# Side rows gathered into one run per fast tile, the running sum in two banks by turns, a third copy buffer

## The reference, cut to what matters

```python
def swiglu(h, w_gate, w_up, w_down):
    return (jax.nn.silu(h @ w_gate) * (h @ w_up)) @ w_down

x = x + 0.5 * swiglu(rms_norm(x, ffn1_norm[l]), ffn1_wg[l], ffn1_wu[l], ffn1_wd[l])
```

## Time and profile before

| quantity | value |
|---|---|
| median of three runs | 2538.85 us |
| the profiled execution | 2539.22 us |
| its span | 2537.4 us |
| TensorE busy | 2515.2 us, 99% of the span |
| VectorE busy | 1875.9 us, 74% |
| ScalarE busy | 1162.6 us, 46% |
| mean granted TensorE clock | 0.999 |

### The profile page before, as it was taken

How to read it: one execution, slowest core, us unless ns; L and a number is a source line. 1 busy time by engine, 2 the same in 40 slices (tenths; PEclk the granted TensorE clock), 3 DMA queues, 4 the chain that set the end, 5 groups by cost and what they waited for, 6 DMA issues and landing times.

```text
span 2537.4 us, 35107 instructions
## 1 busy us (share of the span) xinstructions
PE 2515.2 (99%) x13914; PEld 2186.0 (86%) x13914; DVE 1875.9 (74%) x2579; ACT 1162.6 (46%) x1843; POOL 303.0 (12%) x250
## 2 busy tenths in 40 slices
PE   8999999999999999999999999999999999999999
PEld 7899988888999889999888899997888888788887
DVE  8878877777788677887776778877999786642433
ACT  5444445444444444443553444445577535431332
POOL 4000001320000000000023000000286231100001
PEclk9999999999999999999999999999999999999999
DMA  5333333232333333333423233334332333233332
GB/s 155 98 94 99 99 102 92 76 101 79 104 98 107 114 88 94 100 97 112 108 59 100 84 99 100 97 108 130 82 76 72 125 92 110 83 107 100 92 100 83
DMA packets 489961, 248.32 MB, mean 98 GB/s; under 512 B 41921, under 2 KB 486598, under 8 KB 489542
## 3 DMA queue, kind: packets, MB, share of 16 engines
q1 hardware_dynamic: 489346, 245.76, 33.5%
q10 hardware_dynamic: 452, 0.32, 0.1%
HBM read 241.84 MB, written 4.19 MB: 97 GB/s over the span
## 4 chain that ended last, share of the span: by engine, by line
PE 92%; DVE 4%; ACT 2%; DMA 1%; issue 1%; POOL 0%; DVEq 0%; ACTq 0%
PE bank L725 8%; PE bank L727 8%; PE bank L726 8%; PE bank L804 7%; PE bank L806 7%; PE bank L805 7%; PE psS L829 4%; PE psS L830 4%; PE psS L831 4%; PE psT L725 4%; PE psT L727 4%; PE psT L726 4%; PE psT L875 2%; PE psT L877 2%; PE psT L876 2%; PE psS L725 1%
## 5 line engine op out<-in xcount | busy, mean ns | idle before, releaser
L2001 DVE TENSOR_TENSOR wlo<-raw,whi 128x1024 fp32r<-128x1024 f32 (+1 forms) x274 | 362.8, 1326 | 114.7 <-ACT whi L1426 111.5
L725 PE MATMUL bank<-xhi,whi 128*128 128x512 f32 x888 | 349.4, 393 | 1.4 <-issue 1.4
L726 PE MATMUL bank<-xlo,whi 128*128 128x512 f32 x888 | 345.9, 390 | 0.0
L727 PE MATMUL bank<-xhi,wlo 128*128 128x512 f32 x888 | 345.8, 389 | 0.0
L1426 ACT ACTIVATE whi<-raw 128x1024 fp32r<-128x1024 f32 (+1 forms) x271 | 276.8, 1025 | 130.4 <-PE psT L727 92.4
L1458 ACT ACTIVATE whi<-tw 128x1024 fp32r<-128x1024 f32 x128 | 135.8, 1061 | 271.7 <-PE bank L806 158.9
L804 PE MATMUL bank<-xsh,whi 128*128 128x256 f32 x768 | 216.7, 282 | 1.6 <-issue 1.6
L806 PE MATMUL bank<-xsh,wlo 128*128 128x256 f32 x768 | 217.3, 283 | 0.0
L805 PE MATMUL bank<-xsl,whi 128*128 128x256 f32 x768 | 217.2, 283 | 0.0
L829 PE MATMUL psS<-hhi,whi 128*128 128x512 f32 x512 | 202.3, 395 | 0.0
L830 PE MATMUL psS<-hlo,whi 128*128 128x512 f32 x512 | 202.2, 395 | 0.0
(11 more groups left out here) (586 smaller groups left out, 6424.7 us busy)
## 6 DMA issues: line engine op xcount, KB each, us to landing
raw<-in_ffn_wg SPq DMA_DIRECT2D x88, 512.0 KB
raw<-in_ffn_wu SPq DMA_DIRECT2D x88, 512.0 KB
raw<-in_w_mlp SPq DMA_DIRECT2D x64, 512.0 KB
raw<-in_w_in SPq DMA_DIRECT2D x53, 512.0 KB
raw<-in_ffn_wd SPq DMA_DIRECT2D x48, 256.0 KB
raw<-in_ffn_wd SPq DMA_DIRECT2D x32, 384.0 KB
raw<-in_ffn_wd SPq DMA_DIRECT2D x48, 192.0 KB
raw<-in_ffn_wd SPq DMA_DIRECT2D x48, 128.0 KB
```

Of the source, the lines that this page charges most:

```text
L725: pe.matmul(dest, a, rhs_hi(k), start=start and k == 0, stop=False)
L726: pe.matmul(dest, a, rhs_lo(k), start=False, stop=False)
L727: mm = pe.matmul(dest, b_, rhs_hi(k), start=False, stop=stop and k == tiles - 1)
L2001: dve.tensor_tensor(wlo[:, a:a + n], raw[:, a:a + n], whi[:, a:a + n].bitcast(F32), ALU.subtract).then_inc(s_split, 1)
```

## The change

It does four things. The four side halves become two whole units that stand together (`side` in place of `side_half`), between P5 and P6, so TensorE's list becomes P1 to P5, unit 0, unit 1, P6, P7. The growing sum lies in bank 0 in even windows and in bank 2 in odd ones, so P1 waits only for work of the window before last. The copy after P3 gets its own buffer, `part[2]`. On ScalarE the copy after P5 moves ahead of `sums_hi(w+1, 0)` and `whole_hi(w+1, 0)`; on VectorE line 2158 moves ahead of `whole_lo(w, 1)`, and line 2172 ahead of `side_adds(w, 0)` and `whole_lo(w+1, 0)`. `s_used` counts as follows: P4 one, unit 0 one, P6 two.

```diff
@@ -166,7 +166,7 @@
         cwl = sb("cwl", 2 * S, F32R)
         dwh = sb("dwh", S, F32R)
         dwl = sb("dwl", S, F32R)
-        part = [sb(f"part{i}", QT) for i in range(2)]
+        part = [sb(f"part{i}", QT) for i in range(3)]
         assert at[0] <= nc.sbuf_usable_end, (at[0], nc.sbuf_usable_end)
         top = at[0]
 
@@ -812,11 +812,8 @@
                 def summed(j):
                     return lambda k: (xsh[:, (4 * k + j) * QT:(4 * k + j + 1) * QT], xsl[:, (4 * k + j) * QT:(4 * k + j + 1) * QT])
 
-                def side_half(w, i, half):
-                    unit = SIDES[w][i]
-                    cut = (len(unit) + 1) // 2
-                    for j in (range(cut, len(unit)) if half else range(cut)):
-                        grp, m, k = unit[j]
+                def side(w, i):
+                    for j, (grp, m, k) in enumerate(SIDES[w][i]):
                         if k == 0:
                             if grp or m >= 2:
                                 pe.wait_ge(k_xa, nf * ADDS + grp * KC + m - 1)
@@ -833,19 +830,17 @@
 
                 def fast_window(w):
                     c, q, g = c0 + 4 * (PLAIN + w), q0, nf * FAST + w
-                    bank_a, bank_c, bank_d = bank[0][:, 0:QT], bank[1][:, 0:QT], psT[:, 0:QT]
+                    bank_a, bank_c, bank_d = bank[2 * (w % 2)][:, 0:QT], bank[1][:, 0:QT], psT[:, 0:QT]
 
                     pe.wait_ge(k_lo, 4 * g + 1)
-                    if w:
-                        pe.wait_ge(k_ev, 4 * g - 1)
+                    if w > 1:
+                        pe.wait_ge(k_ev, 4 * g - 5)
                     else:
-                        pe.wait_ge(s_gs, fb + 2 * PLAIN - 1)
+                        pe.wait_ge((s_us if w else s_gs), fb + 2 * PLAIN - 1 + w)
                     terms(bank_a, cwh, cwl, 0, corner(0, 0), True, True).then_inc(k_pe, 1)
                     if w:
                         pe.wait_ge(k_ev, 4 * g - 3)
                     terms(bank_d, cwh, cwl, S, corner(4, 0), True, True).then_inc(k_pe, 1)
-                    pe.wait_ge(k_lo, 4 * g + 3)
-                    side_half(w, 0, 0)
                     pe.wait_ge(k_lo, 4 * g + 2)
                     pe.wait_ge(k_sn, 3 * g + 1)
                     if w == 0:
@@ -856,18 +851,17 @@
                     else:
                         pe.wait_ge(s_us, fb + 2 * PLAIN - 1)
                     terms(bank_c, whi, wlo, S, summed(0), True, True).then_inc(s_used, 1)
-                    side_half(w, 0, 1).then_inc(s_used, 1)
                     pe.wait_ge(k_lo, 4 * g + 4)
                     pe.wait_ge(k_sn, 3 * g + 2)
                     terms(bank_a, whi, wlo, 2 * UNIT, summed(2), False, True, True).then_inc(k_pe, 1)
+                    pe.wait_ge(k_lo, 4 * g + 3)
+                    side(w, 0).then_inc(s_used, 1)
                     pe.wait_ge(s_split, q + c + 4 + RING)
-                    side_half(w, 1, 0)
+                    side(w, 1)
                     pe.wait_ge(k_sn, 3 * g + 3)
-                    terms(bank_a, whi, wlo, 2 * UNIT + S, corner(4, QT), False, True, True).then_inc(s_used, 1)
-                    pe.wait_ge(s_split, q + c + 3 + RING)
+                    terms(bank_a, whi, wlo, 2 * UNIT + S, corner(4, QT), False, True, True).then_inc(s_used, 2)
                     pe.wait_ge(k_ev, 4 * g + 2)
                     terms(bank_c, dwh, dwl, 0, summed(3), False, True, True).then_inc(k_pe, 1)
-                    side_half(w, 1, 1).then_inc(s_used, 1)
 
                 def last_down(m, k0, k1):
                     n, f0 = tiles_in(-1), GROUPS[-1][0]
@@ -1524,21 +1518,24 @@
                     whole_hi(w, 1)
                     act.wait_ge(k_pe, 5 * g + 1)
                     if g:
-                        act.wait_ge(k_ev, 4 * g)
-                    act.activation(part[0][:, :], bank[0][:, 0:QT], ACT.Copy).then_inc(k_sn, 1)
+                        act.wait_ge(k_ev, 4 * g - 3)
+                    act.activation(part[0][:, :], bank[2 * (w % 2)][:, 0:QT], ACT.Copy).then_inc(k_sn, 1)
                     if on:
                         corner_hi(w + 1)
                     act.wait_ge(k_pe, 5 * g + 3)
-                    act.wait_ge(k_ev, 4 * g + 1)
-                    act.activation(part[0][:, :], bank[0][:, 0:QT], ACT.Copy).then_inc(k_sn, 1)
+                    if g:
+                        act.wait_ge(k_ev, 4 * g)
+                    act.activation(part[2][:, :], bank[2 * (w % 2)][:, 0:QT], ACT.Copy).then_inc(k_sn, 1)
+                    act.wait_ge(k_pe, 5 * g + 4)
+                    if g:
+                        act.wait_ge(k_ev, 4 * g - 2)
+                    act.activation(part[1][:, :], bank[2 * (w % 2)][:, 0:QT], ACT.Copy).then_inc(k_sn, 1)
                     if on:
                         sums_hi(w + 1, 0)
                         whole_hi(w + 1, 0)
                     else:
                         ahead(u + 4)
                         ahead(u + 5)
-                    act.wait_ge(k_pe, 5 * g + 4)
-                    act.activation(part[1][:, :], bank[0][:, 0:QT], ACT.Copy).then_inc(k_sn, 1)
                     if on:
                         sums_hi(w + 1, 1)
                     else:
@@ -2152,26 +2149,27 @@
                     t1, t2 = quarter
                     if w:
                         side_adds(w - 1, 1)
-                    whole_lo(w, 1)
                     dve.wait_ge(k_pe, 5 * g + 2)
                     dve.wait_ge(k_sn, 3 * g + 1)
                     dve.tensor_tensor(tmp[1][:, t1], psT[:, 0:QT], part[0][:, :], ALU.add).then_inc(k_ev, 1)
+                    whole_lo(w, 1)
                     if on:
                         corner_lo(w + 1)
                         weight_sums(w + 1)
                         sums_lo(w + 1, 0)
                     else:
                         ahead(u + 4)
+                    dve.wait_ge(k_pe, 5 * g + 4)
+                    dve.wait_ge(k_sn, 3 * g + 3)
+                    dve.wait_ge(s_hl, f)
+                    dve.tensor_tensor(tmp[3][:, t2], bank[1][:, 0:QT], part[1][:, :], ALU.add).then_inc(k_ev, 1)
                     side_adds(w, 0)
                     if on:
                         whole_lo(w + 1, 0)
                     else:
                         ahead(u + 5)
-                    dve.wait_ge(k_pe, 5 * g + 4)
-                    dve.wait_ge(k_sn, 3 * g + 3)
-                    dve.tensor_tensor(tmp[3][:, t2], bank[1][:, 0:QT], part[1][:, :], ALU.add).then_inc(k_ev, 1)
                     dve.wait_ge(s_used, c + 3)
-                    dve.tensor_tensor(tmp[1][:, t2], bank[0][:, 0:QT], inv[:, t2], ALU.mult).then_inc(k_ev, 1)
+                    dve.tensor_tensor(tmp[1][:, t2], bank[2 * (w % 2)][:, 0:QT], inv[:, t2], ALU.mult).then_inc(k_ev, 1)
                     dve.wait_ge(k_ev, 4 * g + 1)
                     dve.tensor_tensor(tmp[1][:, t1], tmp[1][:, t1], inv[:, t1], ALU.mult).then_inc(s_gs, 1)
                     if on:
@@ -2179,7 +2177,7 @@
                     else:
                         ahead(u + 6)
                     dve.wait_ge(k_pe, 5 * g + 5)
-                    dve.tensor_tensor(tmp[3][:, t1], bank[1][:, 0:QT], part[0][:, :], ALU.add).then_inc(k_ev, 1)
+                    dve.tensor_tensor(tmp[3][:, t1], bank[1][:, 0:QT], part[2][:, :], ALU.add).then_inc(k_ev, 1)
                     dve.wait_ge(k_ev, 4 * g + 4)
                     dve.tensor_tensor(tmp[3][:, :], tmp[3][:, :], inv[:, :], ALU.mult).then_inc(s_us, 1)
                     dve.wait_ge(s_us, f + 1)
```

## The result

The changed kernel takes 2639.18 us (median of five runs, 2637.54 to 2639.61) against 2538.68 for the kernel before: a ratio of 1.0393, 95% interval 1.0381 to 1.0405. The forecast was 2636 us in a range of 2620 to 2650. The profiled execution took 2637.56 us with a span of 2635.8, 98.4 us more than the span before.

What follows compares the result with a forecast made beforehand. The prediction took TensorE, busy 99% of the span, as the bound. Stalls, window 0, fewer width changes, reordering and later additions summed as 2539.2 + 100.4 + 3.3 - 3.8 - 3.2 + 0.5 = 2636.4 us, median 2636, range 2620 to 2650.

Steps and rivals of the forecast that it cites:

- The stall at P3: P3 waits for the copy after P1, ending a 5.83 us chain only 4.32 covered: 1.68 us per four-row window, 100.4 total.
- The restart: P3's delayed start and slow second matmul after waiting for the copy: 0.17 us, bounds 0.05 to 0.21.
- Window 0: P3 in each part's first window loses a half's cover: +1.39 us first part, 0.63 each other, 3.3 total.
- Fewer changes between 512 and 256 columns: On TensorE, four runs of side rows per window become one, saving the cost of entering a run: 3.8 us gained.
- The reordered copy and line 2172: In window 12 of each part, P7's wait behind P6 goes: 4 x 0.8 = 3.2 us gained.
- Two banks: P1 no longer waits for line 2174, but nothing was waiting there: nothing gained.
- The third buffer: Separate part[2] removes the wait for line 2158 ahead of the second copy, which was hidden: no gain.
- What now stands closer: VectorE's additions behind line 2172 may come late, tightest in window 8: 0 to 4 us, taken as 0.5.
- Nothing waits: Rival: the copy after P1 ends within 4.32 us of P7's start, leaving only gains, 2532 us; chance 0.04.
- A second wait: Rival: later up-weight landing makes additions hold up unit 1, 12 to 16 waits, +7 to +15 us; chance 0.06.
- The clock falls: Rival: regular TensorE pauses bring the 1.2 GHz level for one product per window, 86 us more; chance 0.04.
- the prediction's own sign: Sign on TensorE that the forecast is wrong: the granted clock leaves 1.00.

Runs made afterwards that it cites:

- experiment 1: Changed kernel with ScalarE's copy after P1 ahead of whole_hi(w, 1) instead of behind it: 2607.6 us.
- experiment 2: Changed kernel with the copy after P1 of the next window placed ahead of hidden_hi on ScalarE: 2546.3 us.
- experiment 3: Changed kernel with the first half of unit 0 put back between P2 and P3: 2556.5 us.
- experiment 4: Changed kernel with the growing sum in bank 0 in every window, as before the change: 2639.4 us.
- experiment 10: Changed kernel with unit 1 moved whole behind P7: 2538.2 us.
- experiment 11: Changed kernel with unit 1 whole behind P7 and, in window 0, unit 0 whole between P2 and P3: 2539.7 us.
- experiment 9: Changed kernel with one more ScalarE copy of 256 columns ahead of whole_hi in windows 1 to 15: 2695.6 us.
- experiment 8: Changed kernel with one more ScalarE copy of 512 columns ahead of whole_hi in windows 1 to 15: 2712.7 us.

## Why the prediction was right, point by point

*The stall at P3.* Forecast 1.68 us in a four-row window, 61 waits in all. The step from P2 to P3 is 3.09 us in place of 1.44, and P3's first step 0.07 longer than the others: 1.72; 1.61 with three rows and 1.83 with five. Over 60 windows that is 102.8 us, where 100.4 was put. The difference is the restart, which took 0.14 + 0.07 = 0.21 us and not 0.17: the upper bound, with the 0.14 of line 2172's row, was right, and the lower bound of 0.05 had no row behind it. Experiments 1, 2 and 3 show that it is this chain.

*Window 0.* P3 waits 1.4 us longer in the first part and 0.5 to 0.6 in the others, 3.1 us for 3.3.

*Fewer changes between 512 and 256 columns.* A four-row window's period is 17.25 us; less the 1.72 of P3's stall that is 15.53, against 15.60 before. With five rows it is 0.07 too, with three rows 0.05: about 4.0 us over 64 windows, put at 3.8. The Trainium skill, "TensorE: Matmul & The Clock Gate", section "Back-to-back issue gap", gives the rule from which the prediction took a gain of nil for an isolated matmul, and sets a stream of weight loads and matmuls apart from it. As a rule for this stream it does not hold here, neither for the change of width nor for the step of 256 columns, 0.120 us in these rows.

*The reordered copy and line 2172.* Window 12's waits went: the periods there had 0.7 to 1.1 us in them, 3.4 us in all, put at 3.2. That the same edit costs 20 us in the old order was not seen: the prediction named what it moves ahead, but not that `sums_hi(w+1, 0)` now stands behind P5. It did no harm because 6.9 us lie between P5's end and P7 in the new order, with units of four rows, against a chain of 3.3; in experiment 10 there are 3.5 us with three rows and 4.2 with four, and still nothing waits; in experiment 11 only P6 lies there in window 0, and P6 and P7 wait. That the forecast held in spite of the oversight is luck in this term.

*Two banks.* Nothing, as said; experiment 4 shows it. The start of line 2174, for which the prediction names, does not stand in those rows; the trace has it at 177.94, 0.20 us after P7's start, as the prediction says. The third buffer has no run of its own; that it brings nothing is not shown.

*What now stands closer.* Window 8 was late behind the additions in two of four parts, by 0.08 and 0.15 us, put at 0.5 in all.

The terms as measured, 102.8 + 3.1 - 4.0 - 3.4 + 0.2, make 98.7 us, against 98.4 between the spans. The median lies 1.6 us above the profiled execution, which the forecast had not foreseen; the section on the hardware has the likely reason.

*The rivals.* "Nothing waits" fell with the chain's 5.82 us. "A second wait" was seen at 0.2 of the 7 to 15 us it was given; it came in experiment 2, at 12.0 us, once the stall at P3 no longer gave the additions their time. "The clock falls" did not come with this kernel's 60 pauses (the profiled execution kept 1.000), but was nearer than its 0.04 said: 0.28 us more of chain brought it. By the prediction's own sign, a granted clock that leaves 1.00, a trace of it was there: three of the five executions have a mean of 0.999 and are 1.8 us longer.

## What to carry to other kernels

Work that looks like filler may be the cover of a chain on other engines: before moving it, add up the chain from the last release to the next wait, in each engine's own order, and compare it with what is left between the two. If a copy or an eviction is all that the matrix engine waits for, first look what stands ahead of it in its engine's list; here the place of one copy was worth 93 us. And an operation moved ahead drags everything behind it after its own wait, so each reordered list wants the same sum again.

## What the runs showed of the hardware

What a pause costs in clock was not in proportion to its length. Sixty pauses of 1.4 to 1.6 us, one in each of the fast tiles' periods of 16 to 19 us, left it at 1.000 in the changed kernel's profiled execution. In experiment 9 the sixty pauses are 1.7 to 1.9 us and it fell with 25 of them, in experiment 8 they are 1.9 to 2.1 us and it fell with 29; in both it also fell once with the 3.0 us of window 0. The length alone does not decide: in experiment 9 none of the 16 pauses of 1.7 us brought it down, 20 of the 32 of 1.8 and 5 of the 12 of 1.9; in experiment 8 10 of 16 at 1.9, 12 of 32 at 2.0 and 7 of 12 at 2.1. What else decides, no run here shows. In a stretch of lower level a 256-column matmul steps by 0.213 in place of 0.120 us; some 16 matmuls fall into one, 16 x 0.093 = 1.5 us lost each time. 26 x 1.5 = 39 us and 30 x 1.5 = 45 us account for the excess of experiments 9 and 8 (39 and 42). The Trainium skill, "TensorE: Matmul & The Clock Gate", section "HAM oscillation", describes a kernel in which every idle stretch, there a wait of about 3 to 5 us for a DMA, lowers the clock for the matmuls behind it. These two runs show the same effect, but at pauses of 1.8 to 2.1 us and with fewer than half of them.

The pause of 3.0 us in window 0 of the first part is the likely reason for the median of the changed kernel: its two executions at 2637.5 us have a mean clock of 1.000, its three at 2639.2 to 2639.6 one of 0.999. Only one of the former has a trace. In the one-bank run, whose profiled execution (2639.3 us) is like the latter, the clock was low once in the fast tiles, from the last half microsecond of that pause on (85.7 to 89.1 us). So the same pause seems to bring the clock down in some executions and not in others, at a cost of some 1.8 us.
